# Order of the first expert loads, page reads, sample rows and conv taps in a decoder step on one core

## What is computed

```
hp = rmsnorm(x) * (1 + scale) + shift          # adaLN from c, per sequence
q, k, v, ca, cg = split(hp @ w_in)             # 5 x 512 columns
q, k = rmsnorm per head of 64; glu = ca * sigmoid(cg)
# stick-breaking attention, 8 heads, strictly causal, no softmax:
a[q, k'] = sigmoid(z[q, k']) * prod over k' < j < q of sigmoid(-z[q, j]);  att = a @ v
# sample group: 8 pages of 128 past keys/values per sequence, by page_table, then its own 4
cv = silu(layernorm(depthwise causal conv of width 31 over glu + b))
x1 = x + gate * (concat(att, cv) @ w_out)
h2 = modulated rmsnorm(x1)
# channel mixer: 16 experts in 4 groups, best group, top 2 in it, weights renormalized
y = x1 + gate2 * sum over 2 experts of w_e * (silu(h2 @ w_gate[e]) * (h2 @ w_up[e])) @ w_down[e]
```

## Time and profile before

| what | value |
|---|---|
| median of 3 runs | 1244.41 us (1244.27 to 1249.14) |
| profiled execution, own time | 1246.21 us |
| its span | 1244.5 us |
| mean granted TensorE clock | 0.972 |
| PE busy | 1150.9 us, 92% |
| DVE / ACT / POOL busy | 602.6 / 337.2 / 252.1 us |
| bytes moved by DMA | 253.37 MB, mean 204 GB/s |
| chain that ended last | PE 79%, DVE 6%, DMA 6%, issue 4%, ACT 3% |

### The profile page before, as it was taken

One profiled execution on the slowest core, in us unless ns is written; L12 is line 12 of the kernel. 1 busy time (PEld: TensorE's weight loads), 2 busy tenths in 40 slices (PEclk: granted clock), 3 DMA queues, 4 the chain that ended last, 5 costly groups with the idle time before them and its releaser, 6 DMA issues.

```text
span 1244.5 us, 19620 instructions
## 1 busy us (share of the span) xinstructions
PE 1150.9 (92%) x6769; PEld 539.9 (43%) x6769; DVE 602.6 (48%) x1161; ACT 337.2 (27%) x713; POOL 252.1 (20%) x312
## 2 busy tenths in 40 slices
PE   6999999999978798998999974899999999999996
PEld 3444444444435566665544443233333333333332
DVE  0010867787689988887965357021221221221212
ACT  2132222122037788887312221000000000000000
POOL 2011101111059500000010001123223233232322
PEclk8999999999988999999999995899999999999999
DMA  9933333322246475654843245997688876977653
GB/s 358 335 134 102 103 102 106 105 81 84 87 150 214 135 225 162 219 159 152 318 144 118 85 150 185 356 398 280 229 283 335 300 286 241 360 252 251 218 215 128
DMA packets 115859, 253.37 MB, mean 204 GB/s; under 512 B 15054, under 2 KB 29518, under 8 KB 114760
## 3 DMA queue, kind: packets, MB, share of 16 engines
q1 hardware_dynamic: 94241, 208.42, 48.1%
q0 software_dynamic: 17568, 39.35, 9.1%
q10 hardware_dynamic: 3984, 4.72, 1.1%
HBM read 399.77 MB, written 39.22 MB: 353 GB/s over the span
## 4 chain that ended last, share of the span: by engine, by line
PE 79%; DVE 6%; DMA 6%; issue 4%; ACT 3%; SPq 0%; POOL 0%; ACTq 0%; DVEq 0%; POOLq 0%
PE bank L1780 20%; PE bank L1457 20%; PE bank L1794 10%; PE bank L1648 8%; PE bank L1437 3%; DMA big<-in_w_gate_dram 2%; PE bank L1491 2%; PE bank L1531 2%; PE bank L1770 1%; PE bank L1313 1%; PE bank L1541 1%; PE bank L1519 1%; DMA big<-in_w_down_dram 1%; DVE big L2060 1%; DMA mid<-in_w_ada_dram 1%
## 5 line engine op out<-in xcount | busy, mean ns | idle before, releaser
L1780 PE MATMUL bank<-big,mid 128*64 128x512 f32 x1232 | 282.2, 598 | 2.0 <-DMA big<-in_w_gate_dram 1.9
L1457 PE MATMUL bank<-big 128*128 128x512 f32 x560 | 249.2, 598 | 0.1
L1457 PEld LDWEIGHTS bank<-big 128*128 128x128 f32 x560 | 103.6, 190 | 131.3 <-issue 131.3
L1953 DVE SCALAR_TENSOR_TENSOR cvT<-low,cw,cvT 128x256 f32<-128x256 f32 x360 | 158.3, 516 | 0.1
L1780 PEld LDWEIGHTS bank<-big,mid 128*64 128x64 f32 x1232 | 87.9, 137 | 159.7 <-issue 158.6
L1794 PE MATMUL bank<-big,mid 128*64 128x512 f32 x608 | 133.7, 592 | 1.1 <-DMA big<-in_w_down_dram 1.1
L2060 DVE TENSOR_TENSOR_SCAN big<-big 128x513 f32<-128x513 f32 (+4 forms) x96 | 91.3, 991 | 15.8 <-ACT big L1086 15.6
L2480 DVE TENSOR_TENSOR xt<-xt,bank 128x512 f32<-128x512 f32 x20 | 13.8, 688 | 152.3 <-ACT xt L1255 152.3
L1794 PEld LDWEIGHTS bank<-big,mid 128*64 128x64 f32 x608 | 44.0, 137 | 87.7 <-issue 87.7
L2499 DVE TENSOR_TENSOR mid<-bank,low 128x512 f32<-128x512 f32 x38 | 24.5, 686 | 115.2 <-PE bank L1794 85.6
L795 POOL TENSOR_TENSOR st<-st,mhalf 128x16 f32<-128x16 f32 (+1 forms) x9 | 25.2, 2801 | 252.6 <-DVE st L1984 243.8
(11 more groups left out here) (341 smaller groups left out, 1344.2 us busy)
## 6 DMA issues: line engine op xcount, KB each, us to landing
big<-in_w_gate_dram SPq DMA_DIRECT2D x42, 2048.0 KB
big<-in_w_up_dram SPq DMA_DIRECT2D x41, 2048.0 KB
big<-in_w_down_dram SPq DMA_DIRECT2D x41, 2048.0 KB
low<-in_w_ada_dram SPq DMA_DIRECT2D x32, 512.0 KB, 4.2
low<-in_cache_v_dram SPq DMA_DIRECT2D x64, 256.0 KB
big<-in_w_in_dram SPq DMA_DIRECT2D x8, 1280.0 KB, 17.2
xt<-in_x_prompt_dram SPq DMA_DIRECT2D x16, 512.0 KB, 4.8
mid<-in_w_ada_dram SPq DMA_DIRECT2D x8, 1024.0 KB, 13.9
```

What stands on the lines that cost most here:

```text
L1457: mm = pe.matmul(bank[:, 4 if cc == 2 else cc, :], hT[:, s, k, :], w_in_sb[:, k, cc * 512:(cc + 1) * 512], start=(k == 0), stop=(k == KD - 1))
L1780: mm = pe.matmul(bank[half, 2 * s + w, :], xgT[:, s, k, half], moving, start=(k == 0), stop=(k == KD - 1))
L1953: c.put(V.scalar_tensor_tensor(out, src, cw[:, ch, tap:tap + 1], out, ALU.mult, ALU.add))
```

## The change

Seven edits, all in the order of work or in where rows lie:

1. The down matrix of pass 0 is issued right behind the up matrix, ahead of SP's two waits.
2. GpSimd waits for `u_mm` 1 (PE's up product of pass 0) before the first `gather_out`.
3. `pages_of(b)` reads the eight page numbers of a sequence once, for keys and values; for sequence 0 between `stage_first()` and `store_turned(7)`, for the others at the head of the loop body.
4. The sample's q, k, v and glu rows lie in `mid` from column 7168 on instead of in buffer 0; with that, three waits for buffer 0 go, and the last prompt conv row store counts on `kv_st[1]`.
5. `evac_page(0)` waits for the prompt's stores only; the load of `w_out`, which overwrites the new rooms, waits for the conv stores.
6. `conv_part(NTP - 1, 3)` goes from the head of the attention; its ten instructions come as two in each of cycles 0 to 4.
7. `TAPS_BY` is new: taps per cycle 1,1,1,1,2,2,2,2,2,2,2,2,2,2,1,1 instead of 2,2,2,2,2,1,2,1,2,1,2,1,2,1,2,1.

The diff, with the re-pointing of the other readers of the sample rows left out:

```diff
@@ -549,19 +552,36 @@
...
                 sp.wait_ge(S["qk_done"], NT)
-                sp.dma_start(ks_out.rearrange("b (j n) -> j b n", j=4), qk_t[:, s, P:2 * P]).then_inc(kv_st[s], 16)
+                sp.dma_start(ks_out.rearrange("b (j n) -> j b n", j=4), smp_qk[:, P:2 * P]).then_inc(kv_st[s], 16)
                 sp.wait_ge(S["v_done"], NT)
-                sp.dma_start(vs_out.rearrange("b (j n) -> j b n", j=4), v_t[:, s, 0:P]).then_inc(kv_st[s], 16)
+                sp.dma_start(vs_out.rearrange("b (j n) -> j b n", j=4), smp_v).then_inc(kv_st[s], 16)
                 for j in range(4):
...
                                          [[TAIL * CC, DB], [CC, DS], [1, P]]),
-                                 glu_t[NS * j:NS * (j + 1), s, 0:P]).then_inc(S["conv_st"], 16)
+                                 smp_glu[NS * j:NS * (j + 1), :]).then_inc(S["conv_st"], 16)
 
...
                     .then_inc(rows_stored[w % 2], 16)
+
+            def pages_of(b):
+                return [sp.value_load(pt[0:1, bass.ds(b * NPG + g, 1)], min_val=0, max_val=NPOOL - 1) for g in range(NPG)]
+
+            def load_keys(b, pages):
+                for g in range(NPG):
+                    sp.wait_ge(S["kt_ps"], 8 * b + g + 1)
+                    sp.dma_start(k_pg[g], ck[bass.ds(pages[g], 1), :, :].rearrange("a p n -> (a p) n"))\
+                        .then_inc(k_in[g], 16)
+
+            def load_values(b, pages):
+                sp.wait_ge(S["s_pv"], b + 1)
+                for g in range(NPG):
+                    sp.dma_start(v_pg[:, g, :], cv[bass.ds(pages[g], 1), :, :].rearrange("a p n -> (a p) n"))\
+                        .then_inc(S["v_in"], 16)
+                sp.wait_ge(kv_st[0], 32 * 5)
+                sp.dma_start(v_new, vs_out[bass.ds(b * DS, DS), :]).then_inc(S["v_in"], 16)
 
@@ -577,6 +597,7 @@
...
                         stage_first()
+                        pages = pages_of(0)
                     store_turned(t - 1)
@@ -587,31 +608,14 @@
...
 
-            def page_of(b, g):
-                return sp.value_load(pt[0:1, bass.ds(b * NPG + g, 1)], min_val=0, max_val=NPOOL - 1)
-
-            def load_keys(b):
-                for g in range(NPG):
-                    page = page_of(b, g)
-                    sp.wait_ge(S["kt_ps"], 8 * b + g + 1)
-                    sp.dma_start(k_pg[g], ck[bass.ds(page, 1), :, :].rearrange("a p n -> (a p) n")).then_inc(k_in[g], 16)
-
-            def load_values(b):
-                pages = [page_of(b, g) for g in range(NPG)]
-                sp.wait_ge(S["s_pv"], b + 1)
-                for g in range(NPG):
-                    sp.dma_start(v_pg[:, g, :], cv[bass.ds(pages[g], 1), :, :].rearrange("a p n -> (a p) n"))\
-                        .then_inc(S["v_in"], 16)
-                sp.wait_ge(kv_st[0], 32 * 5)
-                sp.dma_start(v_new, vs_out[bass.ds(b * DS, DS), :]).then_inc(S["v_in"], 16)
-
-            load_keys(0)
+            load_keys(0, pages)
             store_sample()
             store_mods(NADA - 1)
-            load_values(0)
+            load_values(0, pages)
             with sp.Fori(1, DB) as b:
-                load_keys(b)
-                load_values(b)
+                pages = pages_of(b)
+                load_keys(b, pages)
+                load_values(b, pages)
 
@@ -640,6 +644,7 @@
...
             sp.wait_ge(S["qkT_st"], 32 * NTP)
+            sp.wait_ge(S["conv_st"], 16 * 5)
             sp.wait_ge(S["s_mm"], DB)
@@ -694,6 +699,7 @@
...
             load_w(wu_sb, w_up, wu_in, e0, (0, None))
+            load_w(wd_sb, w_down, wd_in, e0, (0, None))
             sp.wait_ge(S["tiles_ready"], 2)
@@ -704,7 +710,6 @@
...
                          cond=e1[1] != e0[1]).then_inc(wg_in[1], 16)
-            load_w(wd_sb, w_down, wd_in, e0, (0, None))
             sp.wait_ge(S["tiles_ready"], 3)
@@ -899,6 +904,7 @@
...
             pool.wait_ge(S["tok_ready"], 2)
+            pool.wait_ge(S["u_mm"], 1)
             for landed, n0 in zip(x1_st, X1_ST0):
@@ -1060,8 +1066,7 @@
...
             nc.scalar.activation(sq_t[:, 0:2 * P], bank[:, 0, 0:2 * P], ACT.Square).then_inc(S["qk_sq"], 1)
-            act.wait_ge(kv_st[s], 32 * (NTP // 2))
-            nc.scalar.activation(v_t[:, s, 0:P], bank[:, 0, 2 * P:3 * P], ACT.Copy).then_inc(S["v_done"], 1)
+            nc.scalar.activation(smp_v, bank[:, 0, 2 * P:3 * P], ACT.Copy).then_inc(S["v_done"], 1)
             evac_post(NTP - 1)
@@ -1111,9 +1116,8 @@
...
                 if n == 0:
-                    act.wait_ge(kv_st[0], 32 * 5)
-                    act.wait_ge(kv_st[1], 32 * 4)
-                    act.wait_ge(S["conv_st"], 16 * 6)
+                    act.wait_ge(kv_st[0], 32 * (NTP // 2))
+                    act.wait_ge(kv_st[1], 32 * (NTP // 2) + 16)
                 act.wait_ge(S["kt_ps"], 8 + n + 1)
@@ -2043,7 +2047,6 @@
...
             dve.sem_inc(S["qbd_done"], 1)
-            conv_part(NTP - 1, 3)
             c.reset()
@@ -2123,7 +2126,7 @@
...
 
-            TAPS_BY = [2 * cy - max(0, (cy - 4) // 2) for cy in range(CYCLES + 1)]
+            TAPS_BY = [max(cy, min(2 * cy - 4, CYCLES + cy - 6)) for cy in range(CYCLES + 1)]
             assert TAPS_BY[-1] == CW - 5
@@ -2142,6 +2145,8 @@
...
                     ln_sum2(0)
+                if cy < CW - LATE_TAP:
+                    conv_taps(NTP // 2 - 2, (2, 3), LATE_TAP + cy, LATE_TAP + cy + 1)
                 for tap in range(TAPS_BY[cy], TAPS_BY[cy + 1]):
```

More of the change, by code:

```diff
@@ L1363, in turn_post @@
                 for ch in range(NCH if t < NTP else 1):
-                    mm = pe.transpose(bank[:, 7, ch * P:(ch + 1) * P], glu_t[:, s, ch * P:(ch + 1) * P], identf[:, :])
+                    gated = glu_t[:, s, ch * P:(ch + 1) * P] if t < NTP else smp_glu
+                    mm = pe.transpose(bank[:, 7, ch * P:(ch + 1) * P], gated, identf[:, :])
                 mm.then_inc(S["post_ps"], 1)
@@ L1381, in turn_sample_qk @@
                 for j in range(2):
-                    pe.transpose(bank[:, 5 + j, 0:P], qk_t[:, NTP % 2, j * P:(j + 1) * P], identf[:, :])\
+                    pe.transpose(bank[:, 5 + j, 0:P], smp_qk[:, j * P:(j + 1) * P], identf[:, :])\
                         .then_inc(S["post_ps"], 1)
@@ L2009, in _ @@
             dve.wait_ge(S["post_ps"], 3 * (NTP - 2) + 1)
-            V.tensor_tensor(glu_t[:, s, 0:P], bank[:, 3, 0:P], sg_t[:, s, 0:P], ALU.mult)\
+            V.tensor_tensor(smp_glu, bank[:, 3, 0:P], sg_t[:, s, 0:P], ALU.mult)\
                 .then_inc(S["glu_done"], 1)
```

12 lines of the change are left out of this document (7 added, 5 removed).

## The result

| | median of 8 runs | lowest to highest |
|---|---|---|
| before, same chip | 1248.01 us | 1244.17 to 1250.55 |
| after | 1240.55 us | 1239.13 to 1244.75 |

The ratio is 0.9944, 95% interval [0.9929, 0.9959]: 7.0 us faster, [5.1, 8.9]. The forecast was 11.2 us, with a range from 5 us down to 16. The change in time lies inside that range; the time itself (1240.55 against a range up to 1239.5) misses it by 1.1. Part of this miss is the starting point: the median of before is 1248.01 over its eight runs, 3.6 above that of the first three, from which the forecast was counted. The direction was right; the forecast gain is 1.6 times the measured one. A second set of runs of the same change gave 8.7 us (0.9930, [0.9904, 0.9956]). The profiled execution took 1239.21 us, its span is 1237.5.

The account below looks back on a forecast made before the run. PE, busy 92% of the span, was taken as the bound, so only its waits could give: -9.0 (attention head) and -2.2 (expert start) make -11.2, 1233.2 us on the median's scale; range 1228 to 1239.5.

Parts of the forecast that it names:

- Part 1 and 2: Attention head: taps moved off it and sample rows in own rooms bring cycle 3's sample product forward; -9.0 us together.
- its branch (-10.2): Attention head, cycle 3: if GpSimd's wide sums miss the scans, PE's own arrival sets the gain, -10.2 instead of -9.0.
- rival E: Attention cycles 0 to 3: PE's low clock lasts longer, through 422 us costing 19, result 1252 us; chance 0.04.
- Part 3: SP's page numbers read once, a read costing 0.42 us: hidden, sum 0, bounds -0.3 and +1 us.
- Part 4: Start of expert stage: down matrix behind up matrix, first gathers held back; -2.2 us, bounds 0 and -7.7.
- 4.4 of hole less a new hole of 2.2: Expert-stage weight stream: 4.4 us empty between 776 and 787, new hole 787 to 789.2; loads 2.2 us earlier.
- gathers held back change the order, not the bytes: Expert-stage DMA stream: holding the gathers was taken to leave the gain of 2.2 us unchanged.
- the 1.8 lost before: Expert stage, 792.6 to 802.4 us: PE's slow clock after the gate wait costs 1.8 us, which goes with that wait.
- The sum at 850 is the same either way: Expert stage: whether held gathers overtake pass 1's up load or not, PE keeps the same 2.2 us from 850 on.
- The Trainium skill's rule on queues taking turns: Expert stage: engines alternate queues packet by packet, so held gathers overtake pass 1's second up half, making the wait at 802.
- B: Expert stage gives nothing, as a new wait at 820 slows PE's clock, costing up to 3.4; -9.0, 1235.4 us; chance 0.20.
- C: Attention: rebalanced taps or GpSimd's sums eat part of the head's gain; -5 to -7, 1237.5 to 1239.5 us; chance 0.13.

Follow-up runs that it names:

- the other trace with the old attention: Only the two expert-stage edits (down matrix behind the up matrix, gathers held), against the kernel before: 0.9997 [0.9984, 1.0010], median 1249.44 us; attention 232.8 us.
- The rival runs: Full change but first output-row gathers not held, against the kernel before, three sets: 0.9882, 0.9908, 0.9918; medians 1235.11, 1235.25, 1237.97 us.
- the first set: The full change against the kernel before, first measurement: ratio 0.9944, median 1240.55 us, 7.0 us faster.

## Why the prediction was right and wrong

- **Part 1 and 2, -9.0: right in mechanism and size, up to cycle 11.** The lead was 11.1 at the sample turn and 9.2 from cycle 5 on, 0.6 of both from ahead of the attention. DVE's sample product ended at 411.05 (before 422.41), 2.4 us earlier than forecast, mostly because GpSimd's wide sums missed it. Before, the scans ahead of it stretched under those sums (416.73 to 420.76 us):

```profile
416.86 2.84 DVE L2060 TENSOR_TENSOR_SCAN big<-big 128x128 f32<-128x128 f32 x2
419.62 1.69 DVE L2076 TENSOR_TENSOR_SCAN big<-big 128x260 f32<-128x260 f32 x1
```

  After, the two short scans (at 407.54) take 1.17 us and the sample scan (at 408.64) 0.88, and the sums (418.18 to 423.62) fall on two other products:

```profile
419.11 3.37 DVE L2073 TENSOR_TENSOR big<-big 128x512 f32<-128x512 f32 x2
```

  Before, the same two took 1.26 us at 429.09, with no sum beside them. The Trainium skill ("SBUF — State Buffer", on the shared port pair) says that such instructions block each other; the traces agree in that DVE's instructions take longer beside the sums, and its branch (-10.2) was the better figure at that point. But what DVE won there it lost again under the same sums one cycle later, and in the end PE was held by DVE's sample product of cycle 5: for 0.29 us in this trace, where the fall of the clock at 418 had already slowed PE, and for 1.75 to 1.88 us in the five traces without that fall. So DVE set the lead, as forecast, though at a product to which the forecast gave nothing.
- **What the step missed: 1.6 us by a fall of PE's clock at 530 us.** I priced such a fall only in cycles 0 to 3 (rival E) and gave the middle of the stage none. The gain in the traces is small also because the trace of before, from which I counted, has no fall behind the head and the shortest attention of its kind: 230.2 us, against 232.8 in the other trace with the old attention. In the runs the attention edits alone gained 9.1 us, [7.2, 11.0]. That this is so near to the forecast 9.0 is in part luck: both kernels have such falls, and the forecast left out both.
- **Part 3, 0: right as part of the sum, wrong as a reason.** Beside the others it was to cost nothing and gain nothing, and the sum of the attention came out so. But it is not a side issue: without it they give nothing (0.9997). I had costed a read at 0.42 us and asked only about the first sequence's pages; the queue behind them (values, then the next sequence's keys) is what was late.
- **Part 4, -2.2: the step that failed.** In place of -2.2 us the two edits gave +0.3 in the trace (51.2 against 50.9 us behind the first gate product) and -0.4 us, [-2.0, +1.2], in the runs of these edits alone. The sum "4.4 of hole less a new hole of 2.2" was mis-sized in its second term. The new hole is there, of the size forecast: 186 GB/s in 780 to 784, (390 - 186) x 4 / 390 = 2.1 us. But "gathers held back change the order, not the bytes" overlooked that they are what fills the stream while the gate load is being issued: 275 and 349 GB/s in 772 to 780, another 1.6 us. Together 3.7 against 4.4, so the stream won 0.7 and not 2.2 (1.1 by the sum over 36 us above). The rival runs bear it out: without the hold the stream has no hole there and the stretch is 4 us shorter. Nor did PE get even that. The held gathers moved beside pass 1's up load, so its wait for up weights was 4.96 us and not 2, and the one for down weights 0.74 and not 3; its four waits sum to 7.3 us, against 6.9 before. Behind the new wait the clock fell (5.22 for 3.65: 1.6 us), about as much as the 1.8 lost before behind the gate wait, which the text had counted as won at first. Why PE got nothing of the bytes that came earlier is open. "The sum at 850 is the same either way" was not tested. The Trainium skill's rule on queues taking turns ("DMA: Bandwidth & Descriptors", Queues, rings and completion order) fits: the up load issued at 780.10 landed at 800.1, behind a gather issued 10.7 us after it (790.76, landed 7.8 us later).
- **The rivals.** B came nearest: no gain at the experts and the attention's as forecast, less the clock's 1.6; but B's slow clock was to come behind a wait at 820, and it came behind the one at 800. C's figure (-5 to -7) was met by the first set, but its mechanism only in small: four middle cycles took 55.6 us (437.25 to 492.81), against 55.2 (433.68 to 488.87), and of DVE's later taps PE felt the wait in cycle 5. E did not come: at the head the low clock ended at 374 us instead of 384.

## What to carry to other kernels

A wait that orders transfers is paid for by what the DMA engines could have done meanwhile: before holding small gathers back for a big load, check in the windows whether they would have run in a hole, and price the hole as lost bytes. When two waits end near each other, test the parts alone: here 3 + 0 made 9, and without one edit priced at nothing none of it was left, because of what stood two places behind it in the issuing queue. And take a baseline for a stage from several traces; one without a clock fall made this change look 2 us worse. Compare only the part of a stage that the edit can touch: 0.7 of the 1.0 us that the expert stage seemed to lose lay ahead of it.

## What the hardware showed that I had not expected

- PE's clock fell to half for about 3.4 us after stretches in which PE was busy 2.43 of 4 us, and with the same row also did not. A fall cost the attention 1.5 to 1.6 us at 475 or 530 us, about 1.0 at 442 and nothing at 418, where PE would have waited in any case. With eight extra turns in the hole none came at these places in three traces; without them none came in two of nine.
- An SP register read took 0.7 us in a row of eight (value pages), more than the 0.42 that I had worked out for one in front of a key page.
- The two products that met GpSimd's wide sums took 3.37 us instead of 1.26.
